# A two-layer attention and expert-retrieval trunk on one core: one routing weight block is kept on chip from part 0 to part 1

## What is computed

```python
for l in range(DEPTH):                      # 2 layers
    h = rms_norm(x) * (1.0 + sc1) + sh1
    proj = h @ w_in[l]                      # q, k, v, qi, ki, wi, conv input
    ...
    x = x + g1 * (mixed @ w_out[l])
    h2 = rms_norm(x) * (1.0 + sc2) + sh2
    x = x + g2 * peer_ffn(h2, peer_wq[l], peer_sub_keys[l], peer_u[l], peer_v[l])

def block(xb):                              # 128 tokens of peer_ffn
    q = (xb @ w_q).reshape(B, 128, 8, 2, half)            # the routing product
    s = jnp.einsum('bthpd,hpnd->bthpn', q, sub_keys)
    ...                                                   # 16 experts a head, 128 a token
    u = exp_u[e]                                          # gathered rows of 1024
    act = gelu(jnp.einsum('btd,bthkd->bthk', xb, u))
    vv = exp_v[e]                                         # gathered rows again
    return jnp.einsum('bthk,bthkd->btd', g * act, vv)
```

## Time and profile before

| what | value |
|---|---|
| median of three runs | 1730.76 us |
| profiled execution, its own time | 1731.45 us |
| its span, first to last instruction | 1729.6 us |
| PE, DVE, POOL, ACT busy | 60%, 64%, 60%, 16% of the span |
| data moved | 689.90 MB, mean 399 GB/s |
| U and V rows (software queue) | 537.06 MB, 78.3% of 16 engines' time |
| weights (hardware queue) | 151.67 MB, 22.5% |
| chain that ended last | DMA 39%, PE 23%, POOL 16%, DVE 12% |
| mean granted TensorE clock | 0.788 of full speed |

### The profile page before, as it was taken

One profiled execution on the slowest core, in us unless ns is written; L12 is line 12 of the kernel. 1 busy time (PEld: TensorE's weight loads), 2 busy tenths in 40 slices (PEclk: granted clock), 3 DMA queues, 4 the chain that ended last, 5 costly groups with the idle time before them and its releaser, 6 DMA issues.

```text
span 1729.6 us, 18395 instructions
## 1 busy us (share of the span) xinstructions
PE 1040.1 (60%) x6158; PEld 588.0 (34%) x6158; DVE 1105.4 (64%) x3009; ACT 272.9 (16%) x717; POOL 1037.9 (60%) x1224
## 2 busy tenths in 40 slices
PE   7989797306886689513788579611789610005555
PEld 4546675302354166301336146400237200002111
DVE  1977989997218486988216667889513979991000
ACT  2140235201110025300100024400210200000000
POOL 2620535676755664666755675467666777777773
PEclk8989899658998689755889879865899865557888
DMA  9998999999999999999999999999999999999998
GB/s 373 393 359 319 405 401 384 409 409 409 409 409 406 405 403 410 403 409 404 397 400 400 407 398 409 409 409 410 399 407 408 398 402 410 409 410 410 409 409 325
DMA packets 194939, 689.90 MB, mean 399 GB/s; under 512 B 21328, under 2 KB 21344, under 8 KB 194590
## 3 DMA queue, kind: packets, MB, share of 16 engines
q0 software_dynamic: 147840, 537.06, 78.3%
q1 hardware_dynamic: 47006, 151.67, 22.5%
HBM read 687.61 MB, written 1.05 MB: 398 GB/s over the span
## 4 chain that ended last, share of the span: by engine, by line
DMA 39%; PE 23%; POOL 16%; DVE 12%; issue 8%; ACT 1%; SPq 1%; POOLq 0%; DVEq 0%; ACTq 0%
DMA rows<-in_peer_u,u_at 18%; DMA rows<-in_peer_v,v_at 17%; POOL rows L742 8%; PE ps L920 8%; DVE rows L1633 8%; POOL rows L730 7%; PE ps L968 6%; DMA rows<-in_w_ada 2%; PE ps L848 2%; PE ps L862 1%; PE ps L908 1%; DMA wring<-in_peer_v,v_at 1%; PE ps L779 1%; PE ps L773 1%; PE ps L892 1%
## 5 line engine op out<-in xcount | busy, mean ns | idle before, releaser
L730 POOL DMA_INDIRECT rows<-in_peer_u,u_at x512 | 482.4, 942 | 357.6 <-DVE dots L1633 177.1
L1633 DVE CUSTOM_DVE_ANT_0 rows<-rows,ps 128x1024 f32<-128x1024 f32 x512 | 610.4, 1219 | 80.8 <-DMA rows<-in_peer_u,u_at 66.7
L742 POOL DMA_INDIRECT rows<-in_peer_v,v_at x462 | 441.1, 955 | 152.7 <-issue 102.9
L968 PE MATMUL ps<-rows,window 128*32 128x512 f32 x1536 | 241.3, 757 | 142.4 <-DMA rows<-in_peer_v,v_at 142.2
L779 PE MATMUL ps<-ident 128*128 128x128 f32 x228 | 40.5, 349 | 352.6 <-DVE dots L1633 352.6
L779 PEld LDWEIGHTS ps<-ident 128*128 128x128 f32 x228 | 36.0, 185 | 367.5 <-DVE dots L1633 355.5
L920 PEld LDWEIGHTS ps<-hT,wring 128*128 128x128 f32 x1152 | 138.6, 202 | 25.8 <-issue 24.3
L968 PEld LDWEIGHTS ps<-rows,window 128*32 128x32 f32 x1536 | 51.9, 125 | 277.7 <-issue 226.7
L920 PE MATMUL ps<-hT,wring 128*128 128x128 f32 x1152 | 143.7, 287 | 0.0
L1321 ACT ACTIVATE diag_eq<-ident,cwT 128x128 f32<-128x128 f32 x372 | 111.2, 387 | 26.8 <-PE ps L946 25.6
L946 PE MATMUL ps<-diag_eq,hc 128*128 128x128 f32 x744 | 97.5, 293 | 21.8 <-ACT diag_eq L1321 21.8
(11 more groups left out here) (266 smaller groups left out, 1330.8 us busy)
## 6 DMA issues: line engine op xcount, KB each, us to landing
wring<-in_w_ada SPq DMA_DIRECT2D x31, 1024.0 KB, 10.6
wring<-in_w_in SPq DMA_DIRECT2D x30, 1024.0 KB, 11.8
wring<-in_peer_wq SPq DMA_DIRECT2D x28, 1024.0 KB, 9.8
rows<-in_w_ada SPq DMA_DIRECT2D x16, 1024.0 KB, 14.8
wring<-in_w_out SPq DMA_DIRECT2D x13, 1024.0 KB, 17.2
rows<-in_peer_u,u_at POOLq DMA_INDIRECT x512, 14.5
rows<-in_peer_v,v_at POOLq DMA_INDIRECT x462, 11.8
rows<-in_w_in SPq DMA_DIRECT2D x6, 1024.0 KB, 15.9
```

What stands on the lines that cost most here:

```text
L730: pool.indirect_dma_start(row(n), None, u_rows, bass.IndirectOffsetOnAxis(ap=u_at[:, p % 2, k:k + 1], axis=0)).then_inc(row_landed[row_slo ...
L742: pool.indirect_dma_start(row(n), None, v_rows, bass.IndirectOffsetOnAxis(ap=v_at[:, p % 2, tok:tok + 1], axis=0)).then_inc(row_landed[row ...
L968: ins = pe.matmul(ps[32 * g:32 * g + 32, YB + q, :], c, row(n)[:, q * 512:q * 512 + 512], start=a == 0, stop=a == 31)
L1633: dve.tensor_tensor_reduce(out=row(n), in0=row(n), in1=h2_shown, scale=1.0, scalar=0.0, op0=ALU.mult, op1=ALU.add, accum_out=dots[:, k:k + ...
```

## The change

The second load of block 3 of the first layer's `peer_wq` is dropped. Part 0 puts the block into slots 1 and 2, where it already lay, and nothing overwrites it before part 1 has used it. So that the ring can do without slots 1 and 2 until then, three pieces of `cacg` of part 1 go to slots 3, 0 and 10, and the fourth to slot 3 again; `qi` goes to 0 and 3; and from `qk` of part 1 to block 2 of its routing the ring is slots 11, 12, 0 and 3, once the kept v block has been used. Part 1 multiplies blocks 2 and 3 one by one (`proj_turned`) instead of as a pair, with two groups of V rows after the first and two after the second. In part 1 ACT makes the sigmoid ahead of the first diagonals, since `diag_eq` holds weights until `cacg` has been read.

```diff
 SLOTS_OF = {...
+            ("cacg", 1): (3, 0, DIAG_SLOT, 3), ("qi", 1): (0, 3)}
...
+HELD_FOR = {(("v", 0), h): ("v", 1) for h in range(2)}
+HELD_FOR.update({(("vqi", 2), h): ("qi", 3) for h in range(2)})
+HELD_FOR.update({(("wq", p, 3), h): ("qp", p + 1, 3) for p in (0,) for h in range(2)})
...
+                elif b and (("wq", p - 1, 3), 0) in HELD_FOR:      # plan(), part 1
+                    both("wq", p, 2)
+                    job("qp", p, 3)
...
+    def ring_slots(i):
+        for p in (1,):
+            if use_at[(("cacg", p), 0)] <= i < use_at[(("qi", 1) if p == 1 else ("qk", p), 0)]:
+                return (0, 3)
+            if use_at[(("cacg", p), 0)] <= i <= use_at[(("wq", p, 2), 1)]:
+                return (0, 3) + KEPT
+        return range(WSLOTS)
...
+        elif i >= n_ring:
+            slot = next(s for s in order if s in ring_slots(i))
         else:
-            top = WSLOTS if i >= n_ring else KEPT[0] if i >= FIRST_WSLOTS - 1 else FIRST_WSLOTS
+            top = KEPT[0] if i >= FIRST_WSLOTS - 1 else FIRST_WSLOTS
...
-            if uses[i] in vec_count:                               # wait_weight_used
+            if uses[i] in HELD_FOR:
+                b, n = bank(HELD_FOR[uses[i]])
+                eng.wait_ge(full[b], n)
+            elif uses[i] in vec_count:
...
-            def proj_turned(block, name, rhs):
-
-                w = [piece(block, 0), piece(block, 1)]
+            def proj_turned(block, name, rhs, kept=None):
+
+                w = [piece(block, h) if kept is None else kept_piece(kept, h) for h in range(2)]
...
-                        proj_turned_wide(("wqs", p, j), hT,
-                                         [lambda n=n: v_to(p - 1, at[5] + 4 * j + n) for n in (2, 3, 4)])
+                        if j and (("wq", p, 3), 0) in HELD_FOR or j and (("wq", p - 1, 3), 0) in HELD_FOR:
+                            proj_turned(("wq", p, 2), ("qp", p, 2), hT)
+                            v_to(p - 1, at[5] + 4 * j + 2)
+                            v_to(p - 1, at[5] + 4 * j + 3)
+                            kept = ("wq", p - 1, 3) if (("wq", p - 1, 3), 0) in HELD_FOR else None
+                            proj_turned(("wq", p, 3), ("qp", p, 3), hT, kept)
+                            v_to(p - 1, at[5] + 4 * j + 4)
+                        else:
+                            proj_turned_wide(("wqs", p, j), hT,
+                                             [lambda n=n: v_to(p - 1, at[5] + 4 * j + n) for n in (2, 3, 4)])
...
             def project(p):                                        # ACT
 
                 t = p % 2
+                if p == 1:
+                    sigmoid(p)
                 make_diags(p, 0, 1)
-                sigmoid(p)
+                if p > 1:
+                    sigmoid(p)
```

More of the change, by code:

```diff
@@ L98 @@
             ("out", 0, 1): (DIAG_SLOT, 3), ("wq", 0, 0): (5, 6), ("ada", 1, 3): (4, 7, 0, 8), ("wq", 0, 1): (1, LATE_SLOT),
-            ("ada", 1, 4): (2, DIAG_SLOT, 3, 5), ("wq", 0, 2): (0, 6), ("wq", 0, 3): (1, 2)}
+            ("ada", 1, 4): (2, DIAG_SLOT, 3, 5), ("wq", 0, 2): (0, 6), ("wq", 0, 3): (1, 2),
+            ("cacg", 1): (3, 0, DIAG_SLOT, 3), ("qi", 1): (0, 3)}
 def ada_steps(p, where):
@@ L251, in plan @@
             elif b % 2 == 0:
-                both("wqs", p, b // 2)
+                if b and (("wq", p, 3), 0) in HELD_FOR:
+                    both("wq", p, 2)
+                    both("wq", p, 3)
+                elif b and (("wq", p - 1, 3), 0) in HELD_FOR:
+                    both("wq", p, 2)
+                    job("qp", p, 3)
+                else:
+                    both("wqs", p, b // 2)
                 job("s", p, b)
@@ L653, in _ @@
                     done_small = True
[L654 to L657, removed]
+                if use_before[i] is not None:
                     wait_weight_used(sp, use_before[i])
@@ L863, in proj_turned @@
                                         start=k == 0, stop=k == KT - 1)
-                        if (i, k) == (3, 3):
+                        if (i, k) == (3, 3) and kept is None:
                             ins.then_inc(piece_used, 1)
```

## The result

The changed kernel is slower: 1734.38 us (median of 8 runs, 1733.34 to 1738.22) against 1730.9 (8 runs, 1728.07 to 1734.1) in the same session, a ratio of 1.0026 with a 95% interval from 1.0016 to 1.0035, so 2.8 to 6.1 us more. The prediction was 1728.4, with a range of 1725.9 to 1731.6. The profiled execution has a span of 1731.6 where before had 1729.6.

The account below looks back on a forecast made before the run. DMA transfers were taken to bound the kernel from the first U rows to the end. Terms -5.1 + 1.9 + 0.8 = -2.4 us against 1731.45 gave 1729.05, or 1728.4 as a median; range 1725.9 to 1731.6.

Parts of the forecast that it names:

- The bytes: Part 0's V rows: two weight pieces fewer, 2.10 MB, remove 5.1 us of transfer at 408 GB/s, the most the change gives.
- The hole in the V rows: Part 0's V rows near 527: the DMA queue runs empty for 1.3 us, plus 0.6 from POOL's issue pace.
- Sum 1.9 us lost: Part 0's V rows: 1.3 us of empty queue plus 0.6 of slower row issue, leaving 3.2 of 5.1 gained.
- none after 536: Expected sign in part 0's V rows: a GB/s dip near 527 and no dip after 536.
- The late fourth piece: Part 0's U rows: part 1's fourth cacg piece lands at 227.5 after 7.7 us, ending the products 0.8 us late.
- the weak stretch from 264 to 280: Part 0's U rows, DMA at 339 GB/s: has 2.8 us free, into which the slipped loads fit.
- a gap in the U rows near 230 without a late sigmoid: Part 0's U rows: listed as a sign that would show the prediction wrong; no size given.
- No hole: Rival, V rows: deeper row backlog keeps all 5.1 us, 0.8 is paid; -4.3, 1726.5 us; chance 0.25.
- POOL takes the gain: Rival, V rows: POOL's issue pace, as from 572 to 600, eats the saving; no change, 1731.4 us; chance 0.17.
- The fourth piece comes late: Rival, U rows: cacg's fourth piece takes 16 us, DVE stands 9.1 longer; +5.9, 1736.7 us; chance 0.10.
- What costs nothing: Around 231 to 253: diagonals after the sigmoid, qi's second piece and qk's first pieces waiting for v cost 0.

Follow-up runs that it names:

- e4: Changed kernel with part 2's four cacg pieces in slots 0, 3, 1, 2, so the first two need not wait for the kept block's product; 1730.8 us, ratio 1.0006.
- e2: Changed kernel without its slots and sigmoid move: the load is dropped, stand-in weights are multiplied, so one block's scores are wrong; 1729.0 us, 0.9995 of before.
- e9: Changed kernel with part 1's fourth cacg piece in slot 2, loaded before the product begins; one block of scores is wrong; 1732.6 us, 1.0008 of before.
- e10: Kernel before with one edit: in part 1 ACT's sigmoid stands ahead of the sixteen diagonals; 1730.2 us, ratio 1.0000.
- e12: Changed kernel with two of part 0's U dots moved ahead of DVE's wait for the sigmoid; 1732.1 us, 1.0008 of before.
- e8: Changed kernel with part 2's cacg in slots 0, 3, 1, 2 and five U dots ahead of the sigmoid's wait; 1725.9 us, 0.9967 of before.

## Why the prediction was wrong, step by step

**The bytes: right.** 687.8 MB, 2.1 less; e4 has B 4.7 us shorter than before, against 5.1 worked out.

**The hole in the V rows: right in place and cause, wrong in size.** In the changed kernel PE's rows are

```profile
520.44 7.31 PE L883 MATMUL ps<-hT,spread_c 128*128 128x128 f32 x64
527.68 3.64 PE L989 MATMUL ps<-rows,window 128*32 128x512 f32 x32
531.25 7.41 PE L883 MATMUL ps<-hT,wring 128*128 128x128 f32 x64
538.60 3.64 PE L989 MATMUL ps<-rows,window 128*32 128x512 f32 x32
```

The block that I took at 7.2 took 7.31, and everything is 5 later than I placed it, part of which is the U rows' loss. The failed term is "Sum 1.9 us lost": the kernel saved 1.3 of 5.1, so it lost 3.8. I had counted as the hole only the delay of the first new row against an unbroken queue, 1.3, and let rows move at full rate before and after it, but for 0.6. The rows of e2 show that the rate is down for 12 us: 158, 299, 353. The view of the transfers in e2 from 524 to 531, in 40 slices of 0.175 us, shows why:

```profile
GB/s 304 258 257 257 281 211 164 164 117 94 94 70 23 47 23 23 140 234 94 117 211 234 211 328 398 374 375 304 187 281 234 257 281 351 328 375 258 258 211 281
```

The rate runs down over 2 us before the queue is empty near 526.5, and the rows that POOL issues one by one from then on don't bring it back to 410. It ends only when the six loads go out behind the kept product: 412 from 536 on. So "none after 536" held in e2, whose times are those of the prediction; in the changed kernel the whole dip lies later, and so from 528 to 541 or so.

**The late fourth piece: the landing right by luck, the bill wrong.** The chain of waits in the changed kernel: start, length, what. Behind it stand PE's product and DVE's `glu`.

```profile
212.52 6.27 PE ps L941 x32
218.79 0.02 issue
218.81 8.46 DMA wring<-in_w_in
227.27 0.04 issue
227.31 3.85 PE ps L941 x32
231.16 0.02 issue
231.19 0.60 ACT mixed_use L1374
```

```profile
227.31 3.84 PE L941 MATMUL ps<-hT,wring 128*128 128x128 f32 x32 [1.39 <-DMA wring<-in_w_in]
231.87 0.69 DVE L1735 TENSOR_TENSOR hc<-ps,mixed_use 128x512 f32<-128x512 f32 x1 [7.54 <-ACT mixed_use L1374]
```

I landed it at 227.5; it landed at 227.27, but after 8.46 where I took 7.7: it had gone out 1.0 sooner, and the two errors cancel. PE waits 1.39 where I had 0.8, and `glu` 7.54 (7.2 predicted). e9 prices this at 1.8 rather than 0.8. The step that failed stands behind it: "I charge it in full, 0.8: the loads that slip fit into the weak stretch from 264 to 280". They do go there (409 now), but the first dip is 6.0 us and that stretch gives only 2.7 back. I had followed the loads of `qk` as to whether PE would get them in time, and it does; I had not asked what the DMA does between 230 and 238 while SP's queue is held by them. The row slots are full, SP waits for v:

```profile
218.81 12.74 SPq L688 DMA_DIRECT2D wring<-in_w_in  x3
238.05 0.88 SPq L688 DMA_DIRECT2D spread_c<-in_w_in  x2
```

Three pieces go out to 231.5, then none until 238.05. Before, four went out up to 230.54, one each 3.57 us from 219.82, two of them `qk`'s. This is 2.3 us that the sum did not have. I listed "a gap in the U rows near 230 without a late sigmoid" as what would prove me wrong, and gave it no price and no rival.

I had weighed the Trainium skill's rule on double buffering ("Trainium Kernel Development and Optimization", section Best Practices) for the fourth piece alone, and let the rows win. For that piece the runs lie between the two: e9 prices it at 1.8, more than the rows' 0.8 and far less than the whole load of 8.46. What I had not weighed is the rest of the rotation: part 1's `cacg` and `qi` go through two free slots and one borrowed, and all of it together costs 4.1 us in A.

**The rivals.** No hole: refuted. POOL takes the gain: its 572 to 600 stretch is at 409, so not that. The fourth piece comes late: it landed in 8.46, below the 10.1 from which that rival decides, so its sign came true and its mechanism did not. The loss that came was the sum of two smaller ones.

**What costs nothing: right for two terms, wrong for the third.** e10 confirms the sigmoid and the diagonals. The first pieces of `qk` stood under the same heading. They went out at 238.05, where I had 237.4, and PE had them in time, as I said; but the wait for v that I put at nothing is the one to which the 2.3 us above go.

## What to carry to other kernels

In a kernel that the DMA bounds, bytes removed are worth time only if something else may be issued at that moment: list what each queue holds, and what its next entry waits for, through the whole stretch, also where no engine waits. A buffer slot that is kept has a price wherever the other slots were the only supply of loads, here 4.1 us for two slots against the 5.1 of the bytes. Where a dip remains, first look for work that waits only by its order (a load that waits for the wrong slot of four, dots behind a sigmoid), since moving it was free here and gave back more than the change had lost.

## What the runs showed of the hardware

A queue that ran dry cost far more here than the delay of the next row: in e2 about 4.1 us of transfer, where I had worked out a delay of 1.3 us. The rate falls to 158 GB/s and is down for 12 us, 299 and 353, while POOL issues a row every 1.25 to 1.5; it is back, at 412, once SP's six loads are queued too. Why rows alone, issued at that pace, don't bring it back sooner is open.

PE's clock fell after a short wait. In the profiled execution of e12 PE stood 2.10 us for the fourth piece, and the products behind it took 5.46 us for 32 where the changed kernel, after a wait of 1.39, took 3.84. The rows are PE's in e12 and in e8, where the wait was nearly as long, and two stretches of e12 and one of e8, where the granted clock is third from the end:

```profile
227.77 5.46 PE L941 MATMUL ps<-hT,wring 128*128 128x128 f32 x32 [2.10 <-DMA wring<-in_w_in]
229.75 3.84 PE L941 MATMUL ps<-hT,wring 128*128 128x128 f32 x32 [2.00 <-DMA wring<-in_w_in]
```

```profile
229.00:232.00 3.00, 3.00 (x19) 3.00 (x19) 0.00 (x0) 0.00 (x0) 0.00 (x0) 0.62 0.85 313
232.00:235.00 3.00, 3.00 (x17) 2.03 (x16) 0.91 (x2) 1.61 (x5) 0.00 (x0) 1.00 0.26 37
229.00:235.00 6.00, 5.25 (x36) 4.44 (x37) 4.16 (x9) 1.26 (x4) 3.85 (x5) 1.00 0.99 331
```

In e12 the clock is 0.62 of full speed, a mean of its two levels 1.2 and 2.4 GHz, and 1.00 again from 232 on. A load that is late by 0.7 us more thus held up the sigmoid by 1.6 more than that; it was seen in one execution. In e8, after a wait of 2.00, the clock stays at 1.00 and the product takes 3.84, so the length of the wait alone does not tell when it falls.
